# One block for the r, k, v tiles and the gate tiles of a hybrid decoder layer on Trainium2

## The reference, cut to what matters

```python
p = h @ w_in[l]
p_rwkv, p_mla, p_gate = jnp.split(p, [RWKV_COLS, RWKV_COLS + MLA_COLS], axis=-1)
# time mixing (RWKV-7), per channel
p = p + (_shift(p, 1) - p) * mu
r, k, v, wd, ad, gd = jnp.split(p, splits, axis=-1)
w_raw = -jax.nn.softplus(-(w0 + jnp.tanh(wd) @ w_lora_up)) - 0.5
decay = jnp.exp(-jnp.exp(w_raw.astype(jnp.float32)))
a = jax.nn.sigmoid(a0 + ad @ a_lora_up)
kk = heads(k * k_k)
kk = kk / jnp.maximum(jnp.sqrt(jnp.sum(kk * kk, axis=-1, keepdims=True)), 1e-12)
k = k * (1.0 + (a - 1.0) * k_a)
y = _wkv7_scan(r_h, w_h, k_h, v_h, kk, a_h)      # in chunks of 104 tokens
# the gates of the two branches
gate_rwkv, gate_mla = jnp.split(jax.nn.sigmoid(p_gate), 2, axis=-1)
```

## Time and profile before

| | |
|---|---|
| median of three runs | 3690.66 us |
| the profiled execution, span | 3684.4 us |
| median less span (what lies around the span) | 6.3 us |
| TensorE busy | 3527.1 us, 96% of the span |
| VectorE / ScalarE / GpSimd busy | 64% / 36% / 42% |
| mean granted clock of TensorE | 0.990 |
| r, k, v block to gates' block, layer 0 / layer 1 | about 505 to 519 / 2313 to 2326 us |
| gates' block ends, layer 0 / layer 1 | about 743 / 2549 us |

### The profile page before, as it was taken

One profiled execution on the slowest core, in us unless ns is written; L12 is line 12 of the kernel. 1 busy time (PEld: TensorE's weight loads), 2 busy tenths in 40 slices (PEclk: granted clock), 3 DMA queues, 4 the chain that ended last, 5 costly groups with the idle time before them and its releaser, 6 DMA issues. The chain is left out here.

```text
span 3684.4 us, 69094 instructions
## 1 busy us (share of the span) xinstructions
PE 3527.1 (96%) x29239; PEld 3297.9 (90%) x29239; DVE 2374.1 (64%) x2821; ACT 1316.6 (36%) x1900; POOL 1538.0 (42%) x875
## 2 busy tenths in 40 slices
PE   6999999999999999999999999999999999999998
PEld 6867988988898999999987689888889989999998
DVE  2374447665658877777835643585657597777687
ACT  5343124212213444453443520441231144444435
POOL 5364930000742655544444569000026435555341
PEclk9999999999999999999999999999999999999999
DMA  5521866422522222273334248563234122222732
GB/s 121 146 64 53 251 204 187 143 72 58 169 75 76 75 81 76 82 266 121 86 69 136 59 128 260 177 191 100 77 114 130 36 92 81 82 80 81 264 119 85
DMA packets 476187, 439.00 MB, mean 119 GB/s; under 512 B 106027, under 2 KB 401159, under 8 KB 475895
## 3 DMA queue, kind: packets, MB, share of 16 engines
q1 hardware_dynamic: 455640, 383.02, 34.5%
q10 hardware_dynamic: 20255, 51.78, 3.8%
HBM read 297.14 MB, written 137.05 MB: 118 GB/s over the span
## 5 line engine op out<-in xcount | busy, mean ns | idle before, releaser
L234 PE MATMUL psum<-h_hi,w_hi 128*128 128x348 f32 x1632 | 355.3, 326 | 10.7 <-ACT lat_sq L864 3.7
L234 PE MATMUL psum<-h_lo,w_hi 128*128 128x348 f32 x1632 | 348.7, 322 | 0.0
L234 PE MATMUL psum<-h_hi,w_lo 128*128 128x348 f32 x1632 | 347.6, 321 | 0.0
L234 PEld LDWEIGHTS psum<-h_hi,w_hi 128*128 128x128 f32 x1632 | 274.7, 189 | 19.6 <-POOL w_lo L282 4.3
L234 PEld LDWEIGHTS psum<-h_lo,w_hi 128*128 128x128 f32 x1632 | 277.3, 189 | 0.0
L234 PEld LDWEIGHTS psum<-h_hi,w_lo 128*128 128x128 f32 x1632 | 274.9, 188 | 0.0
L3255 POOL TENSOR_TENSOR piece_lo_w<-sum,piece_hi_w 128x512 fp32r<-128x512 f32 x120 | 209.5, 1746 | 141.6 <-ACT piece_hi_w L3557 138.5
L3300 PE MATMUL psum<-t_hi,piece_hi_w 128*128 128x260 f32 x1280 | 258.2, 283 | 5.1 <-issue 2.6
L3300 PE MATMUL psum<-t_hi,piece_lo_w 128*128 128x260 f32 x1280 | 257.3, 282 | 0.0
L3300 PE MATMUL psum<-t_lo,piece_hi_w 128*128 128x260 f32 x1280 | 257.2, 282 | 0.0
L280 POOL TENSOR_TENSOR w_hi<-w_raw,consts 128x1024 fp32r<-128x1024 f32 (+1 forms) x78 | 126.9, 1627 | 295.5 <-PE psum L234 108.8
(11 more groups left out here) (655 smaller groups left out, 9749.7 us busy)
## 6 DMA issues: line engine op xcount, KB each, us to landing
w_raw<-in_w_in SPq DMA_DIRECT2D x68, 512.0 KB, 8.8
wsum<-in_w_down SPq DMA_DIRECT2D x88, 256.0 KB
wsum_scratch<-wsum SPq DMA_DIRECT2D x22, 1024.0 KB
raw_g<-in_w_up SPq DMA_DIRECT2D x40, 512.0 KB, 3.8
raw_v<-in_w_up SPq DMA_DIRECT2D x40, 512.0 KB, 3.9
gate_scratch<-gst ACTq DMA_DIRECT2D x32, 522.0 KB, 3.0
gbuf<-gate_scratch SPq DMA_DIRECT2D x32, 522.0 KB, 3.6
prep_scratch<-prep ACTq DMA_DIRECT2D x8, 2080.0 KB, 8.3
```

The source lines that it names most:

```text
L234: last = nc.tensor.matmul(bank[:, n, :], w(k), x(k)[:, nrange(n)], start=(k == 0 and q == 0), stop=(k == kt - 1 and q == 2))
```

## The change

The two blocks become one, so the barrier between them goes. The first gate tile's weights are loaded right behind the last r, k, v tile's weights, and split on GpSimd behind the last sums; G0 follows the last r, k, v tile on TensorE. The three float32 products of the first pair stand inside G0, in front of its feature tiles 1, 3 and 5, all through `pset[1]`. ScalarE and VectorE get the first pair's steps behind the last tile's copy and shift. In the later pairs each gate tile's number goes up by one, and three gate tiles remain behind the fourth pair instead of four.

```diff
 SyncE
+                load_unit(sp, nt + 2, 0, loaded, split, [(kview(KD), w_in_v[:, :, GATE0:GATE0 + P])])
                 wsum_store(KF - 1)
                 ...
-                for n in (1, 0, 2):
-                    sp.dma_start(rkv[:, n, :], rkv_d[n * RT]).then_inc(next_in, 16)
-                for s in range(2):
-                    sp.wait_ge(split.sem, split.of(nt + s + 1))
-                    sp.dma_start(kview(KD)(w_raw[s]), w_in_v[:, :, GATE0 + s * P:GATE0 + (s + 1) * P]).then_inc(first_in[s], 16)
-                sp.wait_ge(first_in[1], 16)
-                ...
-                sp.wait_ge(next_in, 16 * 4)
+                sp.dma_start(rkv[:, 1, :], rkv_d[RT]).then_inc(k_in, 16)
+                for n in (0, 2):
+                    sp.dma_start(rkv[:, n, :], rkv_d[n * RT]).then_inc(rkv_in, 16)
+                for u in (1, 2):
+                    sp.wait_ge(split.sem, split.of(nt + 1 + u))
+                    sp.dma_start(kview(KD)(w_raw[u % 2]), w_in_v[:, :, GATE0 + u * P:GATE0 + (u + 1) * P]).then_inc(raw_in[u % 2].sem, 16)
 GpSimd
-                pool.wait_ge(first_in[0], 16)
-                pool.wait_ge(used.sem, used.of(nt + 1))
-                split_next(pool, 0, first_hi, first_lo)
+                split_unit(pool, nt + 2, 0, nt // 2 + 1, loaded, hi_done, split, (used.sem, used.of(nt + 1)))
 TensorE
-                for s in range(2):
-                    rows = slice(s * DECAY_LORA, P if s else DECAY_LORA)
-                    pe.wait_ge(acts.sem, acts.of(nt // 2 - 1, f"raw{s}"))
-                    product32(pset[s], [(w_l[rows, :], lora_x[rows, :])]).then_inc(lora_up, 1)
-                keep_warm(7, 3)
+                def first_rows(k):
+                    if k == 1:
+                        pe.wait_ge(lora_in, 32)
+                        pe.wait_ge(apre.sem, apre.of(0, "tanh"))
+                        pe.wait_ge(racts.sem, racts.of(nt // 2 - 1, "raw1"))
+                        pes.did(product32(pset[1], [(w_l[0:DECAY_LORA, :], lora_x[0:DECAY_LORA, :])]), "zw0")
+                    if k == 3:
+                        pe.wait_ge(acts.sem, acts.of(0, "sq0"))
+                        pes.did(product32(pset[1], [(head_ones[:, :], sqn[:, :])]), "ss0")
+                    if k == 5:
+                        pe.wait_ge(dves.sem, dves.of(0, "ssm0"))
+                        pes.did(product32(pset[1], [(w_l[DECAY_LORA:P, :], lora_x[DECAY_LORA:P, :])]), "za0")
+                pe.wait_ge(split.sem, split.of(nt + 3))
+                pe.wait_ge(racts.sem, racts.of(nt // 2 - 1, "raw0"))
+                pes.did(product(pset[0], KD, wtile(w_hi[0], KD), wtile(w_lo[0], KD), hk(h_hi), hk(h_lo), first_rows), "G0")
 ...
-                    gate(g, two, (acts.sem, acts.of(0, f"a{j}")))
-                    gate(g + 1, one, (dves.sem, dves.of(0, f"ssm{j}")))
+                    gate(g + 1, two, (acts.sem, acts.of(0, f"a{j}")))
+                    gate(g + 2, one, (dves.sem, dves.of(0, f"ssm{j}")) if j else (acts.sem, acts.of(0, "g0")))
                     blocks(j, 0)
 ...
-                    gate(g + 2, one, (acts.sem, acts.of(0, f"g{g + 1}")))
+                    gate(g + 3, one, (acts.sem, acts.of(0, f"g{g + 2}")))
                     blocks(j, 2)
-                for u in range(3 * RT, NGT):
+                for u in range(3 * RT + 1, NGT):
 ScalarE
+                raw_out(nt // 2 - 1, 1)
 ...
-                square(0)
+                hi(1)
                 for j in range(RT):
 ...
+                    if j == 0:
+                        mixed_out(nt // 2 - 1, 1)
+                        square(0)
+                        wsum_landed(act)
+                        hi(2)
 VectorE
+                wsum_landed(dve)
                 nc.vector.memset(mid[:, NC:NC + 1], 0.0).then_inc(mid_pad, 1)
 ...
+                lo(1)
 ...
+                    if j == 0:
+                        lo(2)
                     dve.wait_ge(pes.sem, pes.of(0, f"ss{j}"))
 ...
-                lo(NGT - 2)
                 solve_first(RT - 1)
                 lo(NGT - 1)
```

## The result

On the chip on which both kernels were compared, the changed kernel took 3673.68 us (median of four runs, 3666.56 to 3676.53) and the kernel before 3690.89 (four runs, 3688.88 to 3693.61). The ratio is 0.9949, with an interval of 0.9934 to 0.9965. The comparison gains 17.2 us on the medians and 18.5 on the means, where 10.3 were forecast.

The account below looks back on a forecast made before the run. TensorE, with matmuls in 96% of the span, was taken as the bound. Block gain 12.5 less slow start 2.2 gives 10.3 us off: span 3684.4 to 3674.1, median 3690.66 to 3680.4 us; range 3673 to 3688.

Parts of the forecast that it names:

- The gap goes: Between the two blocks, TensorE's idle gap closes: G0 with three products takes 16.6 us, ending 10.5 and 8.3 us earlier per layer.
- The chain inside G0 keeps up: Inside G0, sigmoid, square, shift, scan and norm copy are ready in time: no wait of TensorE or some tenths, 0.2 us taken.
- the moved wait: Rival, chance 0.17: the old TensorE waits, 10.2 us together, stand inside G0 again; 3690.6 us, or 3685.5 with half of them.
- late weights: Rival, chance 0.06: G1's weights come late, ScalarE holds up sigmoid, square and G0; up to 3703.0 us.
- The end of the block: At the gates' block's end, the inverses finish last, 2.8 and 3.5 us behind TensorE; gain 12.5 us instead of TensorE's 18.8.
- The slow start: At the recurrence's start, TensorE's clock falls after idling 4.0 and 4.7 us: 2.2 us more in layer 0, none in layer 1.
- The range: Whole kernel, 3673 to 3688 us: from a fast start in both layers to a good half of the wait come back.

## Why the prediction was wrong, point by point

- **The gap goes.** Held. G0 takes 17.5 us instead of 16.6. The products cost (17.5 - 11.44) / 3 = 2.0 each inside a tile, not 1.65: the row of twelve in the earlier trace rows had them back to back; by difference, some 0.35 more for each product that stands alone among passes of another kind. TensorE's own gain, from the last copy to the end of the fillers, is 9.8 and 8.8 us (10.5 and 8.3 forecast).
- **The chain inside G0 keeps up.** Held: the timeline shows no wait in front of the products, and the square is ready when it is wanted. G1's weights are in time. The rivals of the moved wait and of late weights are out.
- **The end of the block.** Held, and shown by moving the chain: the inverses take over, TensorE idles 4.1 and 4.25 us (4.0 and 4.7 forecast), and the start follows their issue by 3.07 (1.94 + 1.2). The block's gain is 12.6 us between the two first profiles and 11.8 on the means, for 12.5.
- **The slow start.** Held in layer 0, 2.4 us on the means for 2.2. In layer 1 it cost 1.5 for 0: the prediction took the one slow start that it saw there for the rule, and the kernel before also starts there at 1.00 and 0.83. By the Trainium skill (TensorE: Matmul & The Clock Gate, the part on the clock gate) an idle TensorE falls back to 1.2 GHz; the trace agrees behind 4 us, and behind 1.2 to 1.4 us it shows 1.00 in seven starts of fourteen.
- **The step that failed** is the last: "The median lies 6.3 above the span, and I take the same distance: 3690.66 - 10.3". It joined the span of one execution to the median of three others. The distance within an execution is 2.1 us, so the profiled one took some 3686.5 us, near the mean of 3687.3, and the three runs were high. The working gave 3674.1 for the span of the changed kernel, which is 3675.9 with its distance of 1.8; measured were 3675.1 on the mean of 17 runs. Of the 5.3 us by which 3680.4 lies above that, 3690.7 - 3687.3 = 3.4 are the level and 12.1 - 10.3 = 1.8 the gain. So the mechanism was right, and the mis-sized term of the sum is what lies around the span: 6.3 was taken, and 1.8 was measured.
- **The range** was too narrow in the other way as well: "Three runs can tell about 0.2%" was right for a verdict, but the range left out the scatter. With 5 us per execution, the means of four runs each differ by some 3.5 us from chance alone; the first comparison's gain of 18.5 on the means lies 6.4 above the 12.1 of all runs: the four runs of the kernel before were 3.8 higher than its mean, and the four of the changed one 2.5 lower than its own. The range needed some 5 us more at the lower end.
- **The gain itself** stays open by some 4 us: 7.9 in the places of the change, 12.1 in the timed runs.

## What to carry to other kernels

Take the distance between time and span from one and the same execution, and before a forecast of 10 us in 3700 ask how far single executions of the unchanged kernel lie apart. When a gap in front of a block is closed, find the chain that ends the block and move its head forward in the same step: here the place of the last matrices within one tile was worth a further 14.9 us, of which 10 are seen in the block and the start behind it. Small products that depend on one another belong inside a large one: behind it they cost their waits, and in layer 0 as much again at the lower clock that followed.

## What the runs showed of the hardware that was not expected

- Two waits of 1.26 and 1.02 us with 0.98 us of matmuls between them were followed by a clock of 0.50. One wait of 1.28 us at the same place, in the version with the matrices inside G12, was followed by 1.00 over the next 10 us.
- In front of the recurrence, pauses of 4.1 to 4.6 us were always followed by a clock below 1 (eight of eight), pauses of 1.2 to 1.4 us in seven cases of fourteen.
- The same program on one core takes 3677 to 3697 us from one execution to the next, the longer the lower its mean clock. The falls of the clock stand at recurring places of the program, in some executions and not in others, and a change elsewhere in the program went with more of them in one stretch (4 to 5 for 1 to 3) and fewer in another (0 to 1 for 1 to 2).
- A float32 product of six matmuls, put into a tile of another kind of product, adds 2.0 us where twelve back to back took 3.30.
